# First attention of a two-block model: values as the stationary side, weights scaled in place, results kept per pair of heads

## What is computed

```python
s = jnp.where(valid[None, :, None, None], s, -jnp.inf)
m = jnp.maximum(jnp.max(s, axis=-1, keepdims=True), sink)
p = jnp.exp(s - m)
denom = jnp.sum(p, axis=-1, keepdims=True) + jnp.exp(sink - m)
o = jnp.einsum('bnkgqc,bnckd->bnqkgd', (p / denom).astype(v.dtype), v_band)
...
merged = (jax.nn.sigmoid(gate_r) * (y_rnn @ w_o_rnn[layer])
          + jax.nn.sigmoid(gate_a) * (y_att @ w_o_attn[layer]))
```

## Time and profile before

| | |
|---|---|
| timed runs | 2606.21, 2613.46, 2612.14 us, median 2612.14 |
| the profiled execution's own time | 2621.94 us |
| its span in the trace | 2620.0 us |
| TensorE, VectorE, ScalarE busy | 2436.1, 1370.6, 1002.0 us |
| mean granted clock of TensorE | 0.971 |

### The profile page before, as it was taken

One profiled execution on the slowest core, in us unless ns is written; L12 is line 12 of the kernel. 1 busy time (PEld: TensorE's weight loads), 2 busy tenths in 40 slices (PEclk: granted clock), 3 DMA queues, 4 the chain that ended last, 5 costly groups with the idle time before them and its releaser, 6 DMA issues.

```text
span 2620.0 us, 35695 instructions
## 1 busy us (share of the span) xinstructions
PE 2436.1 (93%) x13374; PEld 1676.6 (64%) x13375; DVE 1370.6 (52%) x2587; ACT 1002.0 (38%) x1789; POOL 77.9 (3%) x133
## 2 busy tenths in 40 slices
PE   6999969999999999999979999999999999987999
PEld 3767843443333433334358888888888878876888
DVE  5678732222232222222257778786785666654685
ACT  3644521111111111111145555654654656553553
POOL 0000010000000000000000000000001000000000
PEclk8999969999999999999989999999999999988999
DMA  8753369999999999999955554555555555541553
GB/s 312 252 196 129 102 262 417 417 416 416 418 417 417 417 416 417 417 417 417 417 195 184 180 186 163 177 188 182 184 179 177 187 114 133 141 109 42 168 187 119
DMA packets 310735, 673.69 MB, mean 257 GB/s; under 512 B 8484, under 2 KB 235983, under 8 KB 277728
## 3 DMA queue, kind: packets, MB, share of 16 engines
q1 hardware_dynamic: 307424, 663.66, 67.8%
q0 software_dynamic: 3200, 8.53, 2.2%
HBM read 670.51 MB, written 1.12 MB: 256 GB/s over the span
## 4 chain that ended last, share of the span: by engine, by line
PE 78%; DVE 12%; ACT 6%; issue 3%; DMA 1%; DVEq 0%; ACTq 0%; SPq 0%
PE PS L368 23%; PE PS L1282 17%; PE PS L369 11%; PE PS L1299 9%; PE PS L1270 5%; PE PS L376 5%; DVE WS L322 3%; PE PS L377 2%; ACT WS L318 2%; PE PS L1831 1%; PE PS L1854 1%; DVE LIN L1419 1%; DVE AC L1422 1%; DVE GLU L1415 1%; DVE XG L1411 1%
## 5 line engine op out<-in xcount | busy, mean ns | idle before, releaser
L368 PE MATMUL PS<-HN,WS 128*128 128x512 f32 x1952 | 711.6, 407 | 24.7 <-DVE WS L322 19.9
L322 DVE TENSOR_TENSOR WS<-RAW,WS 128x1024 fp32r<-128x1024 f32 (+1 forms) x452 | 539.6, 1205 | 163.1 <-ACT WS L318 157.4
L369 PE MATMUL PS<-HN,WS 128*128 128x256 f32 x1952 | 553.5, 284 | 0.0
L318 ACT ACTIVATE WS<-RAW 128x1024 fp32r<-128x1024 f32 (+1 forms) x452 | 462.3, 1036 | 86.5 <-PE PS L369 72.4
L1282 PE MATMUL PS<-W,XG 128*64 128x512 f32 x2048 | 448.7, 596 | 10.5 <-DVE XG L1411 10.5
L368 PEld LDWEIGHTS PS<-HN,WS 128*128 128x128 f32 x1952 | 372.7, 191 | 124.4 <-DVE WS L322 23.0
L369 PEld LDWEIGHTS PS<-HN,WS 128*128 128x128 f32 x1952 | 374.9, 192 | 0.3
L1282 PEld LDWEIGHTS PS<-W,XG 128*64 128x64 f32 x2048 | 149.6, 137 | 295.6 <-issue 295.6
L1415 DVE TENSOR_SCALAR GLU<-PS 128x512 f32<-128x512 f32 x32 | 22.1, 692 | 454.3 <-PE PS L1282 454.3
L368 PE MATMUL PS<-MI,WS 128*128 128x512 f32 x704 | 248.9, 399 | 0.0
L1299 PE MATMUL PS<-W,AT 128*64 128x512 f32 x1024 | 226.8, 595 | 22.0 <-ACT AT L1199 22.0
(11 more groups left out here) (342 smaller groups left out, 2636.5 us busy)
## 6 DMA issues: line engine op xcount, KB each, us to landing
W<-in_moe_w SPq DMA_DIRECT2D x192, 2048.0 KB, 14.7
RAW<-in_ffn_w_in SPq DMA_DIRECT2D x88, 1024.0 KB, 5.2
RAW<-in_attn_w_qkv SPq DMA_DIRECT2D x36, 1024.0 KB, 5.2
RAW<-in_ffn_w_out SPq DMA_DIRECT2D x32, 1024.0 KB, 5.0
RAW<-in_w_ada SPq DMA_DIRECT2D x24, 1024.0 KB, 7.8
RAW<-in_w_in SPq DMA_DIRECT2D x22, 1024.0 KB, 5.3
RAW<-in_ffn_w_out SPq DMA_DIRECT2D x16, 768.0 KB, 4.3
RAW<-in_conv_w_in SPq DMA_DIRECT2D x12, 1024.0 KB, 5.2
```

Source lines behind the costliest of these rows:

```text
L318: act_f(split_tile(0, n), raw_tile(n), ACT.Copy).then_inc(hi_done, 1)
L322: vec.tensor_tensor(split_tile(1, n), raw_tile(n), split_tile(0, n).bitcast(f32), ALU.subtract).then_inc(lo_done, 1)
L368: nc.tensor.matmul(both, hi[:, k, :], x2[:, :, kx, :], start=start, stop=False)
L369: ins = nc.tensor.matmul(half, lo[:, k, :], x2[:, 0, kx, :], start=False, stop=stop)
```

## The change

The product with the values turns round: the values are the stationary side and the transposed weights move, so that the result comes out with features on partitions, head x of a pair in partitions 0 to 63 or 64 to 127 of bank 7 and query block b in its columns. The weights have to be divided before the product then, since queries lie along the free axis of the result: `invert(u)` on VectorE forms denominator and inverse and scales the exponentials in place, and `turn_keys` waits for it (`a_scaled`). A pair of heads stays in bank 7 until ScalarE copies it to `AOT` (`a_kept`, steps of the new table `KEPT_AT`: 20, 24, ... 48). `turn_out` and `out` are gone; the split into `YAH` and `YAL` reads `AOT`.

```diff
@@ -560,6 +560,7 @@
+        KEPT_AT = {FIRST + 4 * m + 6: m for m in range(DC)}
@@ -650,6 +651,10 @@   (ScalarE, behind)
+                if s in KEPT_AT:
+                    m = KEPT_AT[s]
+                    act.wait_ge(sem("a_pv"), 4 * m + 4)
+                    act_f(OT[:, m, :], bank[7][:, 0:S], ACT.Copy).then_inc(sem("a_kept"), 1)
                 if 0 <= s - FIRST < NU:
                     exp(s - FIRST)
@@ -664,8 +669,8 @@
-                    act.wait_ge(sem("o_T"), m + 1)
-                    act_f(YAH[:, m, :], bank[5][:, 0:S], ACT.Copy).then_inc(sem("ya_hi"), 1)
+                    act.wait_ge(sem("a_kept"), m + 1)
+                    act_f(YAH[:, m, :], OT[:, m, :], ACT.Copy).then_inc(sem("ya_hi"), 1)
@@ -786,7 +791,7 @@   (TensorE, turn_keys)
-                pe.wait_ge(sem("a_exp"), u + 1)
+                pe.wait_ge(sem("a_scaled"), u + 1)
@@ -798,22 +803,13 @@   (TensorE, weigh)
                 pe.wait_ge(sem("a_ET"), u + 1)
-                if u:
-                    pe.wait_ge(sem("a_out"), u)
+                if u >= 4:
+                    pe.wait_ge(sem("a_kept"), u // 4)
+                h = slice(64 * (x % 2), 64 * (x % 2) + 64)
                 for kb in range(b + 1):
-                    last = nc.tensor.matmul(bank[7][:, 0:HD], ET[b][:, kb * P:(kb + 1) * P],
-                                            VT[:, kb, x // 4 * HD:(x // 4 + 1) * HD], start=kb == 0, stop=kb == b)
+                    last = nc.tensor.matmul(bank[7][h, b * P:(b + 1) * P], VT[:, kb, x // 4 * HD:(x // 4 + 1) * HD],
+                                            ET[b][:, kb * P:(kb + 1) * P], start=kb == 0, stop=kb == b)
                 last.then_inc(sem("a_pv"), 1)
-
-            def turn_out(m):
...
@@ -832,8 +828,6 @@   (TensorE, behind)
-                if s in O_AT:
-                    turn_out(O_AT[s])
@@ -925,6 +919,14 @@   (VectorE)
+            def invert(u):
+                b = u % 2
+                dve.wait_ge(sem("a_sink"), u + 1)
+                o.link(TTN(STAT[:, 3, b:b + 1], STAT[:, 1, b:b + 1], STAT[:, 2, b:b + 1], ALU.add))
+                o.link(vec.reciprocal(STAT[:, 4, b:b + 1], STAT[:, 3, b:b + 1]))
+                e = ES[b][:, 0:(b + 1) * P]
+                TS(e, e, STAT[:, 4, b:b + 1], None, ALU.mult).then_inc(sem("a_scaled"), 1)
@@ -932,15 +934,6 @@   (VectorE, take_weights)
                 vec.tensor_copy(ET[b][:, 0:n], bank[6][:, 0:n]).then_inc(sem("a_ET"), 1)
-                dve.wait_ge(sem("a_sink"), u + 1)
-                o.link(TTN(STAT[:, 3, b:b + 1], STAT[:, 1, b:b + 1], STAT[:, 2, b:b + 1], ALU.add))
-                o.mark(vec.reciprocal(STAT[:, 4, b:b + 1], STAT[:, 3, b:b + 1]))
-
-            def out(u):
...
@@ -959,12 +952,12 @@   (VectorE, behind)
+                if 0 <= s - FIRST - 1 < NU:
+                    invert(s - FIRST - 1)
                 if 0 <= s - FIRST < NU:
                     peak(s - FIRST)
                 if 0 <= s - FIRST - 1 < NU:
                     take_weights(s - FIRST - 1)
-                if 0 <= s - FIRST - 2 < NU:
-                    out(s - FIRST - 2)
@@ -985,7 +978,7 @@
-                    TTN(YAL[:, m, :], bank[5][:, 0:S], YAH[:, m, :].bitcast(f32), ALU.subtract).then_inc(sem("ya_lo"), 1)
+                    TTN(YAL[:, m, :], OT[:, m, :], YAH[:, m, :].bitcast(f32), ALU.subtract).then_inc(sem("ya_lo"), 1)
```

More of the change, by code:

```diff
@@ L536, in mixer @@
         VT = ra("VT", [TT, KV * HD])
-        OT = ra("AOT", [TT, D])
+        OT = ra("AOT", [DC, S])
         rt = Region(tables_at)
@@ L934, in take_weights @@
                 vec.tensor_copy(ET[b][:, 0:n], bank[6][:, 0:n]).then_inc(sem("a_ET"), 1)
-                dve.wait_ge(sem("a_sink"), u + 1)
-                o.link(TTN(STAT[:, 3, b:b + 1], STAT[:, 1, b:b + 1], STAT[:, 2, b:b + 1], ALU.add))
-                o.mark(vec.reciprocal(STAT[:, 4, b:b + 1], STAT[:, 3, b:b + 1]))
-            def out(u):
-                x, b = u // 2, u % 2
-                dve.wait_ge(sem("a_pv"), u + 1)
-                o.wait()
-                TS(OT[:, b, x * HD:(x + 1) * HD], bank[7][:, 0:HD], STAT[:, 4, b:b + 1], None, ALU.mult).then_inc(sem("a_out"), 1)
             def behind(s):
```

## The result

The changed kernel takes 2743.78 us (median of 4, 2742.35 to 2762.38), the kernel before in the same runs 2609.35 us (median of 4, 2606.21 to 2613.46): ratio 1.052, 95% interval 1.048 to 1.056, 134 us slower. The forecast was 2722 us, with a range of its own of 2705 to 2735 and one of eight in ten up to 2745: the time is above the first and just inside the second. Direction and mechanism hold. The excess was forecast at 110 us and is 134.

What follows compares the result with a forecast made beforehand. TensorE, busy 93% of the span, was taken to bound the kernel. The loop's +78 us and the clock's 32 us made +110 us: 2722 us for the median, own range 2705 to 2735, eight in ten 2682 to 2745.

Steps and rivals of the forecast that it cites:

- The wait: TensorE's transposes wait for VectorE's scale behind lo_tile; scale ends 3.41 us after the tile's end, 60 to 90 us idle.
- closed loop: Attention steps: tile, half, splits, sum, reciprocal, scale, transposes, then next tile; no engine runs ahead, 7.16 us a step.
- The rival "not slower": Attention stage: scale comes before tile s's end, about 0.1 us a step gained, 2609 us; chance 5%.
- The turned product: TensorE, between transposes and tile: 128 columns moved instead of 64 add 0.10 us a product; half-width weights count nothing.
- "ScalarE and VectorE set the pace of those steps": Attention steps before the change: these engines, not TensorE, limit them, so lighter instruction lists bring no separate gain.
- The recurrent layer's passes: VectorE between lo_tile and invert, steps 17 to 22: two 2.3 us passes and eight scans, 9.4 us.
- The loop's sum: Attention stage at full clock: 239.5 us against 161.7, so +78 us.
- The clock: TensorE's longer gaps between tiles lower its granted clock: 21 slow tiles at 1.55 us, 32 us.
- "I take two tiles in three, as behind the three gaps": Slow-tile count in the attention stage, from gaps of 3.5 us or longer before the change: 21 of 32.
- The rival with the clock low behind nearly every gap: Attention stage: clock falls behind every gap for most or all of each tile, 2741 to 2776 us; chance 15%.
- The copies: ScalarE's eight new copies into AOT cost nothing under the wait; uncovered, about 0.4 us each, 3 us in all.
- The prediction's row with two pointers: Trace row of tensor_scalar at 128x256, 0.408 us, an upper bound for the scale; neither proves nor refutes two elements a cycle.

Runs made afterwards that it cites:

- the longer scale path: Changed kernel with two more in-place VectorE passes (times 1.0) over the exponentials ahead of the scale: 2774.25 us, ratio 1.063.
- the last kernel: Changed kernel with transposes and product one step later, values padded with zeros to 128 columns, units of a head pair reordered: 2618.35 us, ratio 1.0024.
- the deeper pipeline: Changed kernel with transposes and product one step later, and VectorE's inverse and scaling of u-1 behind the copy of u-2: 2620.65 us, ratio 1.003.
- the scaling in its own step: Changed kernel with inverse and scaling of a unit in the step of its peak and exp, copies to AOT one step earlier: 2623.0 us, ratio 1.004.
- the zeros beside the values: Changed kernel, inverse in the step of its exp, copies a step earlier, values zero-padded to 128 columns; half the heads' results lost: 2647.78 us, stage 167.9 us.
- the kernel with nine more matmuls: Changed kernel with nine useless 128x512 matmuls between scores and transposes of each of the 32 steps: 2696.54 us, ratio 1.033.

## Why the prediction was right in kind and short in size

**The wait.** Right, step by step: from the tile's end to the scale's end 3.31 us (forecast 3.38 for 128 elements), L928 at 0.29 and 0.35 us as taken, 93.3 us of waiting, a little over the 60 to 90 named. That it is a closed loop was shown by the longer scale path, one for one, and that its cause is the place behind `lo_tile` by moving only that. The rival "not slower", if the scale came ahead of the tile's end, came out for those kernels as +21 to +7 us and not at -3: it had left out the product's own price, the copies, and the waits for L928 that stay, 20.9 to 6.8 us (12.0 in the last kernel).

**The turned product.** The sum had +0.16 us a step, for 64 more moving columns, and nothing for the half-width weights. Measured +0.31, all of it from the half width. Over 32 steps this is 5 us more than counted. In the kernels without the long wait the full width takes 2.7 us off a stage that is 8.9 over the kernel before, and in the deeper pipeline 3.9 off 5.2. "ScalarE and VectorE set the pace of those steps" was true of half of them: before, TensorE waited in 16 of the 32 gaps, 14.6 us in all. In tiles 27 to 31 the gaps before are 0.76 and 2.09 us, in which TensorE waits for nothing. There each of its instructions counts. For the scaling in its own step they are 1.07 and 2.39, with the zeros beside the values 0.76 to 0.82 and 2.09 again.

**The recurrent layer's passes.** Counted at 9.4 us. In the kernel with nine more matmuls, which is at full clock but for one tile, the gaps of steps 17 to 22 exceed 4.2 us by 9.2 us together.

**The loop's sum** was 78 us and is 82 to 84, by the kernel with nine more matmuls; the excess is about what the product was short by.

**The clock is the term that was mis-sized.** The forecast put 21 of 32 tiles at 1.55 us too slow, 32 us. The 1.55 us were right and the count was not: it is 28 tiles, 42 us more than in the kernel with nine more matmuls. And a piece was left out: the low clock lengthens the gap too, because the last part of it is TensorE's own. A gap at the low level, in the changed kernel:

```profile
296.46 0.47 PE L800 MATMUL PS<-SM,AES 128*128 128x128 f32 x1 [2.73 <-DVE AES L928]
296.86 1.12 PE L810 MATMUL PS<-AET,VT 128*64 128x128 f32 x4
297.91 0.80 PE L368 MATMUL PS<-HN,WS 128*128 128x512 f32 x1
```

From transpose to tile 1.45 us, where the full clock took 0.84; that gap is 4.81 us and one of the same kind at full clock 4.20. Over the stage this is 8 to 10 us (153.7 us of gaps against 145.5, less 2 for the added work). Loop 82 to 84, tiles 42 and gaps 8 to 10 make the 134; against the forecast's 110 that is 4 to 6 from the loop, 10 from the count and 8 to 10 from the gaps. The step that failed is thus "I take two tiles in three, as behind the three gaps": three gaps are too few to count from, they were shorter than all the new ones, and a gap's length was not the sign. The trace of the kernel before has a third slow tile, which the earlier trace rows leave out, behind a gap of 2.49 us in which TensorE was busy for 1.02:

```profile
210.12:212.61 2.49, 1.02 (x6) 0.74 (x7) 1.92 (x8) 1.19 (x4) 0.00 (x0) 1.00 0.33 106
212.61:217.20 4.59, 4.59 (x19) 3.78 (x18) 2.20 (x5) 2.71 (x3) 0.00 (x0) 0.63 0.50 171
```

The rival with the clock low behind nearly every gap, 2741 us and up, was the closer one.

**The copies** cost nothing, as forecast, but for the reason that the wait is long. Without that cover the waits for them are 8.9 us in one kernel, and moving them a step earlier saves 5 us in another, in place of 3.

## What to carry to other kernels

When a wait moves to an instruction that itself stands behind the waiting engine's last result, count the whole way round and not the added instruction: here 0.3 us of new work on VectorE became 2.6 us a step, and the clock added more than half as much again. Place such an instruction ahead of what depends on the tile, or pipeline it by one more step; that gave back 113 to 125 of 134 us, and 128 together with the full-width product. Look for each edit's price once more without the big wait, since the wait hides the prices of the others, and look at what else waits for the engine whose list was reordered; and where TensorE waits for nothing, a product half as wide is not a cheaper one.

## What the runs showed of the hardware

- An fp32 tensor_scalar from SBUF to SBUF with one pointer scalar took 0.29 us at 128 elements and 0.35 at 256: 0.06 us for 128 more. The Trainium skill, "VectorE: DVE Perf Modes", section "The perf-mode tier table", gives this operation two elements a cycle. The rows are in keeping with that, as far as a ratio can be: the scalar_tensor_tensor of L917, with two tensor inputs and one of them in PSUM, took 0.28 and 0.42 us, 0.14 for 128 more, about twice as much. The prediction's row with two pointers had left it open.
- More matmuls made the kernel 47 us faster: 288 matmuls of 0.40 us each, in idle time, left one slow tile where there were 28. The Trainium skill, "TensorE: Matmul & The Clock Gate", section "Why this matters for your kernels", names idle gaps between bursts of matmuls as what brings the lower clock back; the trace agrees. It is still 85 us slower than the kernel before, so filling a wait is no match for taking it away.
- The lower clock lengthens the small matmuls between tiles as well: the two products (four instructions in the trace) and the way to the next tile took 1.05 us in place of 0.58.
- A product on 64 of the 128 columns cost 0.31 us more than one on all of them, between full-width matmuls (0.84 against 0.53 us from transpose to tile).
